# Ten units of seven half-size products a layer instead of nine in the feed-forward part of a two-layer decoder trunk in float32

## The chip, the cores and the metric

The kernel runs as one program on one core of a Trainium2 chip. The metric is the device time of one execution in microseconds (us); lower is better. Five engines run side by side, each working through its own list of instructions in order: TensorE (PE, with its weight loads shown as PEld), VectorE (DVE), ScalarE (ACT), GpSimd (POOL) and SyncE (SP). They meet only at semaphores. DMA queues move data between the chip's memory and the on-chip memory.

## The reference, cut to what matters

Each of two layers mixes (retention, spatial gating, dilated attention, an output product) and then runs a gated feed-forward block. The change touches the gate and up products of the last two lines:

```python
D_MODEL, SEQ, DEPTH, D_FF = 1024, 512, 2, 2816
for l in range(DEPTH):
    ...
    x = x + merged @ w_o[l]
    h = rms_norm(x, g_ffn[l])
    gate, up = jnp.split(h @ w_gate_up[l], 2, axis=-1)
    x = x + (jax.nn.silu(gate) * up) @ w_down[l]
```

Everything is float32, and h is 512 x 1024. Gate and up have 2816 columns each, that is 22 tiles of 128, which the kernel takes in 11 pairs of tiles.

## The kernel before, in words

**Float32 in parts.** Each operand of a product is stored as a high part (a copy in the type fp32r, which the matmuls read) and a low part (the rest). A product is three matmuls: high by high, high by low, low by high (L823, and L841 to L843). ACT makes the high part by a copy, DVE the low part by a subtraction. This holds for weights (`split_high` on ACT at L1011, `split_low` on DVE at L1215, per slab of 8 blocks of 128 x 128) and for activations.

**Tiles.** A layer is a list of tiles (`tiles_of_layer`), and tile i writes PSUM bank i modulo 2. So TensorE can't start tile i before tile i-2 has been read out of its bank (`wait_evacuated`). A plain gate or up tile (`fgate`, `fup`) is 8 blocks by 3 matmuls of 512 columns. For the first tile of the feed-forward block the normalization factor isn't ready, so plain tiles are computed from the gain-scaled x, and scaled afterwards by `norm_rstd` (L1322 for gate, L1355 and L1356 for up, where the second multiplies by the gate).

**Seven products.** A pair of gate tiles and a pair of up tiles together are a product of a 2 x 2 blocked input (halves of the tokens by halves of the 1024 inner columns) with a 2 x 2 blocked weight matrix. For a "quick" unit the kernel takes the seven products of Strassen's scheme (in Winograd's form) instead of eight. Each of the seven steps is one tile of 8 blocks by 3 matmuls of 256 columns:

```python
QUICK = (("a11", "b11"), ("s2", "t2"), ("a12", "b21"), ("s1", "t1"), ("s3", "t3"), ("s4", "b22"), ("a22", "t4"))
A11B11, S2T2, A12B21, S1T1, S3T3, S4B22, A22T4 = range(7)
ONTO = {A12B21: A11B11, S4B22: S1T1}
BY_SCALAR = (A11B11, A12B21, S1T1)
```

t1 to t4 are sums of weight blocks. POOL makes them ahead by adding DMAs in the chip's memory (L673, L675), eight DMAs a unit, one unit after the other, starting after the tile `rv 0` of the same layer. A11B11, A12B21 and S1T1 are read out by ACT (L1054 and L1064 are copies, L1060 is the silu), the other four by DVE (L1292 S2T2, L1295 and L1298 S3T3, L1301 and L1306 S4B22, L1308 A22T4). S2T2's read-out adds the copy of A11B11.

**Input of the units.** It is the same for all units of a layer, and made once, beside the plain tiles. DVE writes the normalized x (`normed`, 8 tiles, L1366), and the sums s1 to s4 of its quarters (`input_sum`, L1381; s2 from s1, and s4 from s2). ACT makes the high part of a11, a12, a22 and s1 to s4 (`part_high`, L1160), DVE the low part (`part_low`, L1386). In the first quick unit of a layer each of the seven tiles waits for the low part of its own input. The parts of a12 and a22 are stored over `h_high` and `h_low`, which plain tiles read, so their high parts wait for the last plain tile.

**Order.** `schedule` writes one list of steps by hand, and each engine takes its own instructions from it in that order. For tile i the list holds: the matmuls, `split_high` of the weights for the tile two further on, `pre[i]`, the read-out `evac`, `split_low`, and `post[i]`. The 4 gate and 4 up tiles of the 2 plain pairs come first (`PLAIN_PAIRS`), then units 2 to 5, then the down product over their 12 tiles, then units 6 to 10 and the second down product. SP loads slab s into one of 3 raw slots once slab s-3 has been split (L712); the slots of the split parts are 3 too.

Of the kernel before, what the change touches and what calls it, by code (L numbers as in the profile page):

```python
# [36 lines left out]
KT = D_MODEL // P  # L37
BLK = SEQ // P
FF_BLOCKS = (12, 10)
PLAIN_PAIRS = 2  # L40
PAIRS = D_FF // P // 2
QUICK_UNITS = range(PLAIN_PAIRS, PAIRS)
DILATIONS = ((128, 1), (512, 4), (2048, 16))
# [17 lines left out]
def tiles_of_layer():  # L61
# [18 lines left out]
    for half in range(2):  # L80
        if half == 0:
            for j in range(2 * PLAIN_PAIRS):
                t += [("fgate", 0, j), ("fup", 0, j)]
# [15 lines left out]
A11B11, S2T2, A12B21, S1T1, S3T3, S4B22, A22T4 = range(7)  # L99
# [4 lines left out]
AT = {t: i for i, t in enumerate(TILES)}  # L104
# [89 lines left out]
def schedule():  # L194
    pre = {i: [] for i in range(len(TILES))}
    post = {i: [] for i in range(len(TILES))}
# [43 lines left out]
    for n in range(KT):  # L240
        post[AT["proj", 1, n]] += [("high", "m", n), ("low", "m", n)]

        for tile, which in ((AT["wo", n], 1), (AT["down", 1, n], "next")):
# [3 lines left out]
            if n == KT - 1:  # L247
                pre[tile] += [("load_sqrt",)]
    for j in range(2 * PLAIN_PAIRS):
        post[AT["fup", 0, j]] += [("high", "f", 0, j), ("low", "f", 0, j)]  # L250
    for u in QUICK_UNITS:
        post[AT["quick", u, S4B22]] += [("high", "f1", u), ("low", "f1", u)]
        post[AT["quick", u, A22T4]] += [("second", u), ("high", "f2", u), ("low", "f2", u)]
    post[AT["fup", 0, 0]] += [("normed", n) for n in range(3)]
    post[AT["fgate", 0, 1]] += [("normed", n) for n in range(3, 7)]
    post[AT["fup", 0, 1]] += [("normed", 7), ("part_high", "a11"), ("part_low", "a11")]
    post[AT["fgate", 0, 2]] += [("input_sum", "s1"), ("input_sum", "s2"), ("part_high", "s2")]
    post[AT["fup", 0, 2]] += [("part_low", "s2"), ("part_high", "s1")]
    post[AT["fgate", 0, 3]] += [("part_low", "s1"), ("input_sum", "s3"), ("part_high", "s3")]
    post[AT["fup", 0, 3]] = [("part_high", "a12"), ("part_low", "s3")] + post[AT["fup", 0, 3]]  # L260
    post[AT["quick", PLAIN_PAIRS, A11B11]] += [("part_low", "a12")]
    post[AT["quick", PLAIN_PAIRS, S2T2]] += [("input_sum", "s4"), ("part_high", "s4"), ("part_low", "s4")]
    post[AT["quick", PLAIN_PAIRS, S1T1]] += [("part_high", "a22"), ("part_low", "a22")]

    post[AT["down", 1, KT - 2]] += [("fill_split",), ("split_high", "next", 0), ("split_low", "next", 0)]
    pre[AT["down", 1, KT - 1]] += [("split_high", "next", 1), ("split_low", "next", 1)]
# [32 lines left out]
STAT_AT, BCAST_AT = 3, 6  # L299
AFTER_NORM = (AT["k", 0, 0], AT["fgate", 0, 0])  # L300
STEPS = schedule()


# [1357 lines left out]
```

## Time and profile before

| | |
|---|---|
| median of 3 runs | 1927.08 us (1926.92 to 1927.63) |
| the profiled execution, its own time | 1928.07 us |
| its span in the profile | 1926.3 us |
| granted TensorE clock, mean | 0.999 of full speed |
| TensorE busy | 1902.9 us, 99% of the span |
| VectorE busy | 1236.6 us, 64% |
| ScalarE busy | 854.4 us, 44% |
| GpSimd busy | 97.0 us, 5% |

The profiled execution took 1.77 us more than its span, and lies 1.0 us over the median of the runs. Times of the trace count from the start of the span. Matmuls are pipelined and their ends are modelled in the rows, so the distance from one start to the next is what it takes of TensorE's time. In the same way the next instruction of DVE or ACT can start a little before the last has ended.

### The profile page before, as it was taken

How to read it: one execution, taken by the hardware profiler on the slowest of the kernel's cores; microseconds unless marked ns; L12 is line 12 of the kernel's file. 1: busy time of each engine (PE TensorE's matmuls, PEld its weight loads, DVE VectorE, ACT ScalarE, POOL GpSimd, SP SyncE). 2: the span in 40 equal slices, each digit the busy share in tenths (PEclk: the TensorE clock that was granted, in tenths of full speed). 3: DMA queues.
4: the chain of work that ended last, by engine and by line, in shares of the span. 5: the costliest groups of instructions: out<-in, count | busy, mean ns of one | idle time of the engine just before them, and what ended most of it. 6: DMA issues, size and time to landing. Idle time of an engine off the chain costs nothing. (4 is left out here: it accounts for less than half of the span.)

```text
span 1926.3 us, 26698 instructions
## 1 busy us (share of the span) xinstructions
PE 1902.9 (99%) x10664; PEld 1703.1 (88%) x10664; DVE 1236.6 (64%) x1633; ACT 854.4 (44%) x1194; POOL 97.0 (5%) x148
## 2 busy tenths in 40 slices
PE   7999999999999999999999999999999999999999
PEld 6888888888888899899888888888888888998998
DVE  6666756745666787267576666677366667863775
ACT  5444444434234455255445444344343344542554
POOL 0000001111111000000000000011111110000000
PEclk9999999999999999999999999999999999999999
DMA  5322247777777356356333222577777773553663
GB/s 190 83 81 84 78 121 197 192 207 202 214 206 198 99 158 182 102 183 198 122 108 87 74 78 79 138 198 188 216 193 199 200 206 106 176 157 109 204 204 126
DMA packets 85897, 295.68 MB, mean 153 GB/s; under 512 B 20368, under 2 KB 20624, under 8 KB 84624
## 3 DMA queue, kind: packets, MB, share of 16 engines
q1 hardware_dynamic: 73104, 218.49, 36.4%
q0 software_dynamic: 12672, 75.51, 17.3%
q8 instruction: 85, 1.39, 0.3%
q14 instruction: 36, 0.29, 0.1%
HBM read 291.79 MB, written 77.66 MB: 192 GB/s over the span
## 5 line engine op out<-in xcount | busy, mean ns | idle before, releaser
L1011 ACT ACTIVATE w_high<-raw 128x1024 fp32r<-128x1024 f32 x396 | 418.1, 1056 | 813.3 <-PE bank L823 685.7
L823 PE MATMUL bank<-h_high,w_high 128*128 128x512 f32 x1472 | 570.1, 387 | 12.8 <-DVE h_low L1220 11.3
L1215 DVE TENSOR_TENSOR w_low<-raw,w_high 128x1024 fp32r<-128x1024 f32 x396 | 482.8, 1221 | 123.3 <-ACT w_high L1011 117.5
L823 PE MATMUL bank<-h_low,w_high 128*128 128x512 f32 x1472 | 559.2, 380 | 0.0
L823 PE MATMUL bank<-h_high,w_low 128*128 128x512 f32 x1472 | 559.1, 380 | 0.0
L823 PEld LDWEIGHTS bank<-h_high,w_high 128*128 128x128 f32 x1472 | 279.2, 190 | 55.9 <-issue 9.4
L823 PEld LDWEIGHTS bank<-h_high,w_low 128*128 128x128 f32 x1472 | 279.0, 190 | 39.8
L823 PEld LDWEIGHTS bank<-h_low,w_high 128*128 128x128 f32 x1472 | 279.2, 190 | 38.3
L823 PE MATMUL bank<-in_high,w_high 128*128 128x512 f32 x672 | 255.0, 379 | 0.0
L823 PE MATMUL bank<-in_low,w_high 128*128 128x512 f32 x672 | 254.7, 379 | 0.0
L823 PE MATMUL bank<-in_high,w_low 128*128 128x512 f32 x672 | 254.7, 379 | 0.0
L1322 DVE TENSOR_TENSOR scaled<-bank,norm_rstd 128x512 f32<-128x512 f32 x128 | 93.7, 732 | 108.3 <-PE bank L823 107.8
L841 PE MATMUL bank<-s_high,w_high 128*128 128x256 f32 x576 | 158.4, 275 | 0.0
L842 PE MATMUL bank<-s_low,w_high 128*128 128x256 f32 x576 | 158.4, 275 | 0.0
L843 PE MATMUL bank<-s_high,w_low 128*128 128x256 f32 x576 | 158.4, 275 | 0.0
L823 PEld LDWEIGHTS bank<-in_high,w_high 128*128 128x128 f32 x672 | 127.0, 189 | 18.3 <-DVE in_low L1413 0.4
L823 PEld LDWEIGHTS bank<-in_high,w_low 128*128 128x128 f32 x672 | 127.0, 189 | 18.0
L823 PEld LDWEIGHTS bank<-in_low,w_high 128*128 128x128 f32 x672 | 127.0, 189 | 17.8
L843 PEld LDWEIGHTS bank<-s_high,w_low 128*128 128x128 f32 x576 | 110.6, 192 | 0.0
L842 PEld LDWEIGHTS bank<-s_low,w_high 128*128 128x128 f32 x576 | 110.6, 192 | 0.0
L841 PEld LDWEIGHTS bank<-s_high,w_high 128*128 128x128 f32 x576 | 110.6, 192 | 0.0
L1345 DVE TENSOR_TENSOR xT<-bank,xT 128x512 f32<-128x512 f32 x32 | 22.1, 691 | 125.3 <-PE bank L823 125.3
(156 smaller groups left out, 2253.1 us busy)
## 6 DMA issues: line engine op xcount, KB each, us to landing
raw<-weights SPq DMA_DIRECT2D x325, 512.0 KB, 4.0
weight_sums<-weights POOLq DMA_DIRECT2D x108, 512.0 KB, 6.1
raw<-weight_sums SPq DMA_DIRECT2D x72, 512.0 KB, 3.5
weight_sums<-weight_sums POOLq DMA_DIRECT2D x36, 512.0 KB, 4.0
turned<-rows SPq DMA_DIRECT2D x3, 768.0 KB, 7.0
xT<-x_t SPq DMA_DIRECT2D x8, 256.0 KB, 5.6
decay_sb<-decay SPq DMA_DIRECT2D x8, 256.0 KB, 4.5
out_t<-xT SPq DMA_DIRECT2D x8, 256.0 KB, 6.4
```

The source lines that it names most:

```text
L823: return pe.matmul(o, w, m, start=start, stop=stop)
L841: pe.matmul(part, wh, hi, start=k + c == 0 and not onto, stop=False, skip_group_check=onto)
L842: pe.matmul(part, wh, lo, start=False, stop=False, skip_group_check=onto)
L843: last = pe.matmul(part, wl, hi, start=False, stop=k == 3 and c == 1, skip_group_check=onto)
L1011: act.activation(w_high[:, PART_SLOT[s], :, :], raw[:, s % RAW_SLOTS, :, :], ACT.Copy).then_inc(part_high_w.sem, 1)
L1215: dve.tensor_tensor(w_low[:, PART_SLOT[s], :, :], raw[:, s % RAW_SLOTS, :, :], w_high[:, PART_SLOT[s], :, :], ALU.subtract).then_inc(part_ ...
L1322: dve.tensor_tensor(*operands, ALU.mult).then_inc(tile_stored.sem, 1)
L1345: dve.tensor_tensor(x, src.rearrange("p (t a i) -> p i a t", a=2, i=2), x, ALU.add).then_inc(tile_stored.sem, 1)
```

## The change

It sets `PLAIN_PAIRS` to 1. Gate and up tiles 2 and 3 of each layer are no longer plain tiles but a unit (unit 1) of seven products, first of ten. The down product reads the outputs of that unit in place of theirs. The host lays the weights out accordingly. The steps that make the units' input are spread over other tiles: before they stood behind six tiles of the plain eight, from `fup 0 0` to `fup 0 3`, and behind three of the first unit; now they stand behind three of four plain tiles and two of the first unit.

```diff
-PLAIN_PAIRS = 2
+PLAIN_PAIRS = 1
...
-    post[AT["fup", 0, 0]] += [("normed", n) for n in range(3)]
-    post[AT["fgate", 0, 1]] += [("normed", n) for n in range(3, 7)]
-    post[AT["fup", 0, 1]] += [("normed", 7), ("part_high", "a11"), ("part_low", "a11")]
-    post[AT["fgate", 0, 2]] += [("input_sum", "s1"), ("input_sum", "s2"), ("part_high", "s2")]
-    post[AT["fup", 0, 2]] += [("part_low", "s2"), ("part_high", "s1")]
-    post[AT["fgate", 0, 3]] += [("part_low", "s1"), ("input_sum", "s3"), ("part_high", "s3")]
-    post[AT["fup", 0, 3]] = [("part_high", "a12"), ("part_low", "s3")] + post[AT["fup", 0, 3]]
-    post[AT["quick", PLAIN_PAIRS, A11B11]] += [("part_low", "a12")]
-    post[AT["quick", PLAIN_PAIRS, S2T2]] += [("input_sum", "s4"), ("part_high", "s4"), ("part_low", "s4")]
-    post[AT["quick", PLAIN_PAIRS, S1T1]] += [("part_high", "a22"), ("part_low", "a22")]
+    post[AT["fup", 0, 0]] += [("normed", n) for n in range(5)]
+    post[AT["fgate", 0, 1]] += [("normed", n) for n in range(5, 8)]
+    post[AT["fgate", 0, 1]] += [("part_high", "a11"), ("part_low", "a11"), ("input_sum", "s1"), ("input_sum", "s2"),
+                                ("part_high", "s2")]
+    post[AT["fup", 0, 1]] = [("part_low", "s2"), ("part_high", "a12"), ("part_low", "a12")] + post[AT["fup", 0, 1]]
+    post[AT["fup", 0, 1]] += [("part_high", "s1"), ("part_low", "s1"), ("input_sum", "s3"), ("part_high", "s3")]
+    post[AT["quick", PLAIN_PAIRS, A11B11]] += [("part_low", "s3"), ("input_sum", "s4"), ("part_high", "s4")]
+    post[AT["quick", PLAIN_PAIRS, S2T2]] += [("part_low", "s4"), ("part_high", "a22"), ("part_low", "a22")]
```

## Rows read from the trace of the kernel before

**Rows 1.** The page: busy time, share of the span and instructions of each engine.

```profile
PE 1902.9 (99%) x10664; PEld 1703.1 (88%) x10664; DVE 1236.6 (64%) x1633; ACT 854.4 (44%) x1194; POOL 97.0 (5%) x148
```

**Rows 2.** Waits of PE, whole span: waiter, releaser, us in total, times, longest.

```profile
PE bank L823 <- DVE h_low L1220: 11.3, 5, 8.7
PE bank L841 <- issue: 3.5, 2, 1.7
...
PE bank L841 <- ACT sq L1054: 1.3, 2, 0.6
```

**Rows 3.** Timeline of PE, layer 0: start us, us, instruction, [idle before <-releaser].

```profile
661.73 0.38 PE L823 MATMUL bank<-h_high,w_high 128*128 128x512 f32 x1
...
682.45 0.27 PE L841 MATMUL bank<-a_high,w_high 128*128 128x256 f32 x1
...
687.70 0.28 PE L843 MATMUL bank<-s_high,w_low 128*128 128x256 f32 x1
689.71 0.35 PE L841 MATMUL bank<-h_high,w_high 128*128 128x256 f32 x1 [1.74 <-issue]
...
708.45 0.28 PE L843 MATMUL bank<-s_high,w_low 128*128 128x256 f32 x1
709.36 0.38 PE L841 MATMUL bank<-h_high,w_high 128*128 128x256 f32 x1 [0.64 <-ACT sq L1054]
```

**Rows 4.** Windows: us, busy of PE, PEld, DVE, ACT, POOL, clock, DMA share, GB/s.

```profile
661.70:682.40 20.70, 20.70 (x97) 18.12 (x97) 18.27 (x20) 9.98 (x12) 0.00 (x0) 1.00 0.34 109
682.40:703.20 20.80, 19.06 (x170) 18.88 (x169) 18.23 (x20) 12.98 (x16) 0.00 (x0) 1.00 0.47 134
722.80:741.60 18.80, 18.80 (x171) 18.80 (x170) 14.25 (x17) 10.66 (x13) 0.00 (x0) 1.00 0.65 199
```

**Rows 5.** Timeline of DVE beside the plain tiles of layer 0.

```profile
654.77 0.84 DVE L1410 TENSOR_TENSOR in_low<-prod,in_high 128x512 fp32r<-128x512 f32 x1
655.52 2.07 DVE L1366 SCALAR_TENSOR_TENSOR normed<-xT,vec,norm_rstd 128x512 f32<-128x512 f32 x3
657.51 0.68 DVE L1322 TENSOR_TENSOR scaled<-bank,norm_rstd 128x512 f32<-128x512 f32 x1
658.11 1.21 DVE L1215 TENSOR_TENSOR w_low<-raw,w_high 128x1024 fp32r<-128x1024 f32 x1
659.25 2.73 DVE L1366 SCALAR_TENSOR_TENSOR normed<-xT,vec,norm_rstd 128x512 f32<-128x512 f32 x4
661.93 0.69 DVE L1355 TENSOR_TENSOR tmp<-bank,norm_rstd 128x512 f32<-128x512 f32 x1
662.66 0.69 DVE L1356 TENSOR_TENSOR prod<-tmp,work 128x512 f32<-128x512 f32 x1
663.60 1.23 DVE L1215 TENSOR_TENSOR w_low<-raw,w_high 128x1024 fp32r<-128x1024 f32 x1 [0.24 <-DVE prod L1356]
...
666.16 1.21 DVE L1386 TENSOR_TENSOR a_low<-normed,a_high 128x1024 fp32r<-128x1024 f32 x1
...
669.41 1.22 DVE L1381 TENSOR_TENSOR input_sum<-normed 128x1024 f32<-128x1024 f32 x1
670.66 1.22 DVE L1381 TENSOR_TENSOR input_sum<-input_sum,normed 128x1024 f32<-128x1024 f32 x1
```

**Rows 6.** Timeline of ACT around the first unit of layer 0.

```profile
682.15 1.06 ACT L1160 ACTIVATE s_high<-normed 128x1024 fp32r<-128x1024 f32 x1 [3.04 <-DVE normed L1381]
683.12 1.05 ACT L1011 ACTIVATE w_high<-raw 128x1024 fp32r<-128x1024 f32 x1
...
686.59 0.58 ACT L1054 ACTIVATE sq<-bank 128x512 f32<-128x512 f32 x1
```

**Rows 7.** Timeline of POOL: the same issue in the last two rounds of layer 0.

```profile
577.07 0.81 POOL L673 DMA_DIRECT2D weight_sums<-weights  x1 [3.92 <-DMA weight_sums<-weight_sums]
...
614.51 0.81 POOL L673 DMA_DIRECT2D weight_sums<-weights  x1 [3.73 <-DMA weight_sums<-weight_sums]
```

**Rows 8.** Timeline of PE at the start of the kernel, behind its broken stretch.

```profile
18.76 0.61 PE L823 MATMUL bank<-h_low,w_high 128*128 128x512 f32 x1
...
22.15 0.40 PE L823 MATMUL bank<-h_high,w_high 128*128 128x512 f32 x1
```

## The prediction

> **What bounds the kernel now.** I read the busy shares first: TensorE is busy for 99% of the span, VectorE for 64%, ScalarE for 44% [rows 1]. So time comes off where TensorE has less to stream, and comes on wherever it has to wait. The list of its waits is the second view: 11.3 us at the start of the kernel, and then only a few, among them two of 1.7 us (3.5 in all) and two of 0.6 at the seven products [rows 2], one of each a layer. The timeline of TensorE says where these are [rows 3]. The plain tiles run without a break from 661.73 to 682.45. The first unit's A11B11 and S2T2 follow, then TensorE stands from 687.81 (687.70 plus one matmul of 0.11) to 689.71, 1.9 us, and its first pair is 0.1 slow: 2.0 in all. The second unit loses 0.8 at the same place (708.56 to 709.36). The windows [rows 4] show the other side: while the plain tiles 2 and 3 run, VectorE is busy for 18.27 us of 20.70, and in the first unit for 18.23 of 20.80, against 14.25 of 18.80 in a unit further on. It is there that the input of the units is made. VectorE, hardly noticed on the page, is nearly full in just the stretch from which the change takes tiles.
>
> **Less streaming.** A plain pair is 4 tiles x 24 matmuls = 96. From 661.73 to 682.45 there are 96, so 0.2158 us each and 20.72 a pair [rows 3]. A unit is 7 x 24 = 168 matmuls of 256 columns. The first 48 go from 682.45 to 687.81, 0.1117 each [rows 3]; a unit is 18.76, which the undisturbed window confirms (171 starts in 18.80) [rows 4]. The difference is 1.96 us a layer, 3.9 for both. The Trainium skill ("TensorE: Matmul & The Clock Gate", Back-to-back issue gap) gives columns by 2.4 GHz plus 2.5 ns, 109.2 ns for 256 columns; the trace disagrees with 111.7. By the page a unit would be 18.3 us and the gain 4.7 instead of 3.9. I take the rows.
>
> **Other work of the extra unit.** A unit has 14.25 us of VectorE and 10.66 of ScalarE under 18.80 of TensorE [rows 4], and each is free for the rest, so it costs nothing in the steady stretch. The three more slabs a layer bring three more loads by SP, one per tile of 2.7 us, into slots that wait for VectorE's split, so they are early where VectorE is late. POOL makes a tenth round of sums: 37.4 us [rows 7]. Its rounds now end some 6 us behind 614.51, then at about 658, and the tenth unit's weights are wanted after more than 100 us of further tiles, so this is hidden; the new first unit's sums are made first of all. If that cover were gone the cost would be the 37 us, but nothing points to it. I take 0 for all of this.
>
> **The moved preparation.** This is the main term. Before, the parts for A11B11 had until 682.45. Now TensorE has finished `fup 0 1` at 661.73 and wants them there, 20.7 us sooner. Nothing of VectorE's preparation is dropped. I therefore walk the new list from the point where both agree, 655.5 [rows 5]. The pitches, start to start, are from rows 5: 0.66 a `normed` (four in 2.68), 0.6 a read-out of a gate tile, 1.14 a weight split or a low part, 1.2 a sum, 1.66 the two instructions of an up tile until the next can start (661.93 to 663.60), 0.75 a plain tile's low part. On ScalarE a high part or weight split has a pitch of 0.97 and a duration of 1.06, a copy out of a bank takes 0.58 [rows 6].
>
> 1. VectorE: five `normed` to 658.8, gate read-out to 659.4, weight split to 660.6, three `normed` to 662.6, low part of a11, done at 663.8. ScalarE has the high part long before. **A11B11 starts at 663.9 instead of 661.7: 2.1 us of wait.** It ends at 666.6.
> 2. VectorE: s1 at 663.7, s2 at 664.9, which ends at 666.1. Only then comes the read-out of `fup 0 1` (ready since 661.9) to 667.7. ScalarE, which is held by s2, makes its high part from 666.2 and the weight split from 667.1 to 668.2. VectorE: weight split at 668.2, low part of s2 at 669.3, done at 670.6. **S2T2 starts at 670.7, having been possible at 666.6: 4.0.** It ends at 673.4.
> 3. VectorE: low part of a12 at 670.5, of the plain product at 671.6, of s1 at 672.4, sum s3 from 673.5 to 674.7. On ScalarE the high part of s3 stands behind that sum, and behind it, in order, are the weight split and the copy of A11B11 out of its bank, which A12B21 needs: 674.8, 675.7, and the copy from 676.7 to 677.3. **A12B21 starts at 677.4: 4.0.** It ends at 680.1. The added wait is thus one of ScalarE for VectorE's sum, with TensorE queued behind the copy.
> 4. VectorE: weight split at 676.8 (held by ScalarE), low part of s3 at 677.9, sum s4 at 679.1, and only then the read-out of S2T2, from 680.3 to 681.0, though ready since 673.5. **S1T1, which writes the same bank, starts at 681.1: 1.0.** It ends at 683.8.
> 5. ScalarE: high part of s4 at 680.4, then two weight splits and the high part of a22, and the silu of A12B21 from 684.2 to 684.8. **S3T3 starts at 684.9: 1.1.** The rest of the unit has what it wants and ends at 693.0.
>
> The waits sum to 12.2 in the first unit. In the second the wait for the copy stays; I take 0.3, from 0 and the 0.8 of before. That is 12.5 against 2.8 before, 9.7 more a layer, of which the streaming gives back 2.0. A layer grows by 7.8, and since both layers have the same rows, the kernel by 15.6. TensorE has nothing left beside these stretches that could take the delay in. 1928.07 + 15.6 = 1943.7 for the execution that was profiled. The median of the runs is 1.0 lower, so I forecast **1942.7 us**.
>
> **A bound from both sides.** Of the trace, nothing shows how ScalarE and VectorE interleave in the new order. Where ScalarE held up nobody, VectorE's own list would still set S1T1's start: less 0.5 at its split at 668.2 and 2.1 at the one at 676.8. S1T1 would start at 678.5, and S3T3 at most 1.1 sooner still, so 3.7 less a layer: +4.1, or +8 for both. From above: each of the dozen hand-overs of the walk may take 0.1 more, 1.2 a layer.
>
> **Rivals.** *The clock falls.* At the start TensorE had waits of 0.3 to 1.5 us between 13 and 18.5, then the matmuls from 18.76 to 22.15 ran at 0.43 us each, 8 of them, in which 15.7 would have run at 0.216 [rows 8]: 1.7 us lost, at the lower of the two levels, 1.2 instead of 2.4 GHz. Waits of 4.0 us are longer. But of the five tiles of the walk the first four are followed by a wait: S2T2, slowed by 1.7, ends at 675.1, before 677.4, and A12B21 ends at 681.8, 0.7 behind S1T1's start, which the wait of 1.1 behind S1T1 takes back. So in the likeliest case it costs nothing. If a low stretch falls on S3T3 and what follows, 1.7 a layer come on top: 1946.1. The Trainium skill (same page, Why this matters for your kernels) warns that idle gaps between bursts bring the clock back to half; no row of the middle of this kernel shows it, since the wait of 1.9 us left the granted clock at 1.00 [rows 4].
>
> *VectorE's list alone counts*, ScalarE is in time: the bound above, 1927.1 + 8 = 1935 at the extreme, about 1939 if half of it holds.
>
> *The preparation is hidden, and the kernel is faster.* The place is A11B11 to A12B21: their parts would have to be there at 661.7, 664.4 and 667.1. Then the waits of the first unit stay as before and 3.9 come off: 1923.2. It needs VectorE to be done with s2's low part 6.2 us sooner than the walk says. Against it: VectorE has hardly a gap in the walk to 674, and 18.27 of 20.70 were busy with this before [rows 4].
>
> *It doesn't do what it says*: the constant is used wherever tiles, sources and units are listed, so this has no share.
>
> **How the numbers follow.** Forecast 0.76; clock 0.12; VectorE alone 0.09; hidden 0.03. The forecast's own spread is the hand-overs, -1.5 to +2.4. The range goes from 1938, by the bound without ScalarE's part, to 1947, by the clock. A difference under 0.2% (3.9 us) is about what a measurement of this kernel can't tell from none. The hidden case lies at that edge, so it gives 0.02 to faster and 0.01 to the same; the other three are all slower, 0.97.
>
> **What would show it.** In the profile after: TensorE's list of waits gets about 20 us longer, at the seven products alone; per layer waits of about 2, 4, 4, 1 and 1 us before the first five tiles of unit 1, for VectorE's low parts (L1386) and ScalarE's copy (L1054); VectorE without a break from 655 to 674; units from the third on 18.8 us apart; 96 fewer matmuls of 512 columns at L823 and 56 more at each of L841 to L843 in a layer. It is wrong if A11B11 follows `fup 0 1` at once, if the wait before A12B21 is short, or if waits show at later units.

## The result, and the profile after

The changed kernel takes 1943.06 us, median of 4 runs (1942.69 to 1945.36), against 1927.31 us before (4 runs, the three of the table above and one more): a ratio of 1.0085, 95% interval 1.007 to 1.01. It is 15.8 us slower. 1942.7 us was forecast.

The first lines of the page of the changed kernel (busy time, share, instructions; against [rows 1]):

```profile
span 1940.9 us, 27042 instructions
...
PE 1907.2 (98%) x10808; PEld 1712.1 (88%) x10808; DVE 1244.3 (64%) x1641; ACT 861.4 (44%) x1204; POOL 108.2 (6%) x164
```

144 more matmuls: 112 more on each of the three lines of the seven products (336), less 192 of 512 columns. VectorE's and ScalarE's totals hardly move. These totals don't say why the kernel is slower; the waits do.

Waits of TensorE in the changed kernel, whole span (waiter, releaser, us in total, times, longest; against [rows 2]; its line numbers are 2 lower from L258 on):

```profile
PE bank L839 <- issue: 10.2, 4, 3.9
PE bank L821 <- DVE h_low L1218: 10.1, 3, 8.2
PE bank L839 <- ACT sq L1052: 4.9, 3, 2.2
...
PE bank L839 <- ACT work L1058: 0.5, 2, 0.3
```

At the seven products the list grew from 4.8 to 15.6 us. Where they are, and which tile they delay, the timeline of TensorE in the changed kernel shows, layer 0 (start, us, instruction, idle before; against [rows 3]):

```profile
660.30 0.38 PE L821 MATMUL bank<-h_high,w_low 128*128 128x512 f32 x1
662.66 0.35 PE L839 MATMUL bank<-a_high,w_high 128*128 128x256 f32 x1 [1.98 <-issue]
...
665.30 0.28 PE L841 MATMUL bank<-a_high,w_low 128*128 128x256 f32 x1
669.49 0.55 PE L839 MATMUL bank<-s_high,w_high 128*128 128x256 f32 x1 [3.91 <-issue]
...
673.53 0.28 PE L841 MATMUL bank<-s_high,w_low 128*128 128x256 f32 x1
675.97 0.58 PE L839 MATMUL bank<-h_high,w_high 128*128 128x256 f32 x1 [2.16 <-ACT sq L1052]
...
680.30 0.28 PE L839 MATMUL bank<-s_high,w_high 128*128 128x256 f32 x1
...
682.87 0.28 PE L841 MATMUL bank<-s_high,w_low 128*128 128x256 f32 x1
683.43 0.38 PE L839 MATMUL bank<-s_high,w_high 128*128 128x256 f32 x1 [0.28 <-ACT work L1058]
...
697.92 0.38 PE L839 MATMUL bank<-h_high,w_high 128*128 128x256 f32 x1 [0.83 <-ACT sq L1052]
...
730.26 0.28 PE L839 MATMUL bank<-a_high,w_high 128*128 128x256 f32 x1
```

Here `fup 0 1` ends at 660.52. In the kernel before it ended at 661.73; the 1.2 us come from the start of the kernel: one and the same wait ends at 27.97 in the kernel before and at 26.75 here, since the first wait is 0.5 shorter (8.2 against 8.7) and the clock stayed at 1.00 where it was at 0.66 before (window 18 to 23). The walk of the prediction, less 1.2, stands beside the rows:

| tile of the first unit | walk less 1.2 | start measured | us that TensorE lost before it |
|---|---|---|---|
| A11B11 | 662.7 | 662.66 | 2.1 |
| S2T2 | 669.5 | 669.49 | 4.1 |
| A12B21 | 676.2 | 675.97 | 2.3, and 1.5 in S2T2 by the clock |
| S1T1 | 679.9 | 680.30 | none, but 1.7 in A12B21 by the clock |
| S3T3 | 683.7 | 683.43 | 0.5 |

The losses sum to 12.2 us, as in the walk. In layer 1 the first unit lost as much: from the end of `fup 0 1` to the start of S4B22 are 25.68 us there and 25.69 in layer 0.

The last row printed starts the fourth unit (730.26). From the end of `fup 0 1` to it are 69.74 us, over three units. The same tiles of the kernel before, one plain pair and two units, ran from 661.73 to the start of its third unit at 722.87: 61.14 us. The layer grew by 8.6. In layer 1 the same stretch grew by 7.7 (1622.56 to 1691.38 against 1615.20 to 1676.33). 16.3 less the 1.2 at the start, and 0.5 less behind the last of these points, is the 14.6 by which the span grew.

VectorE in the changed kernel, beside the last plain tiles and the first unit (timeline; against [rows 5]), has one gap between 652.5 and 673.3:

```profile
654.31 3.40 DVE L1364 SCALAR_TENSOR_TENSOR normed<-xT,vec,norm_rstd 128x512 f32<-128x512 f32 x5
...
661.34 1.22 DVE L1384 TENSOR_TENSOR a_low<-normed,a_high 128x1024 fp32r<-128x1024 f32 x1
662.48 1.22 DVE L1379 TENSOR_TENSOR input_sum<-normed 128x1024 f32<-128x1024 f32 x1
663.73 1.23 DVE L1379 TENSOR_TENSOR input_sum<-input_sum,normed 128x1024 f32<-128x1024 f32 x1
664.87 0.68 DVE L1353 TENSOR_TENSOR tmp<-bank,norm_rstd 128x512 f32<-128x512 f32 x1
665.59 0.69 DVE L1354 TENSOR_TENSOR prod<-tmp,work 128x512 f32<-128x512 f32 x1
667.02 1.23 DVE L1213 TENSOR_TENSOR w_low<-raw,w_high 128x1024 fp32r<-128x1024 f32 x1 [0.74 <-ACT w_high L1009]
668.17 1.22 DVE L1384 TENSOR_TENSOR s_low<-input_sum,s_high 128x1024 fp32r<-128x1024 f32 x1
```

The low part of a11 ends at 662.56 and A11B11 starts at 662.66; the low part of s2 ends at 669.39 and S2T2 starts at 669.49. The rows of TensorE put both waits down to "issue", which means that the profile shows no releaser; these times show it. ScalarE's timeline shows the step that holds A12B21 (against [rows 6], where the same high part cost nothing):

```profile
673.43 1.06 ACT L1158 ACTIVATE s_high<-normed 128x1024 fp32r<-128x1024 f32 x1 [4.00 <-DVE normed L1379]
674.39 1.04 ACT L1009 ACTIVATE w_high<-raw 128x1024 fp32r<-128x1024 f32 x1
675.34 0.58 ACT L1052 ACTIVATE sq<-bank 128x512 f32<-128x512 f32 x1
```

It waits 4.0 us for VectorE's sum s3, with the weight split and the copy of A11B11 behind it in its list. The copy of A11B11 (L1052) ends at 675.92, A12B21 starts at 675.97.

### The profile page after: what moved, and what is told of

Read it like the earlier page. It is cut to its first block and busy times, and to the rows that moved or that the text cites. A ratio compares the mean times of both kernels' runs of the same rounds, so it can differ in the third digit from the quotient of the medians.

```text
span 1940.9 us, 27042 instructions
## 1 busy us (share of the span) xinstructions
PE 1907.2 (98%) x10808; PEld 1712.1 (88%) x10808; DVE 1244.3 (64%) x1641; ACT 861.4 (44%) x1204; POOL 108.2 (6%) x164
## 5 line engine op out<-in xcount | busy, mean ns | idle before, releaser
L821 PE MATMUL bank<-h_high,w_high 128*128 128x512 f32 x1408 | 545.5, 387 | 11.6 <-DVE h_low L1218 10.1
L821 PE MATMUL bank<-h_high,w_low 128*128 128x512 f32 x1408 | 534.6, 380 | 0.0
L821 PE MATMUL bank<-h_low,w_high 128*128 128x512 f32 x1408 | 534.6, 380 | 0.0
L821 PEld LDWEIGHTS bank<-h_high,w_high 128*128 128x128 f32 x1408 | 266.9, 190 | 52.3 <-issue 8.8
L839 PE MATMUL bank<-s_high,w_high 128*128 128x256 f32 x640 | 178.0, 278 | 6.7 <-issue 6.2
L840 PE MATMUL bank<-s_low,w_high 128*128 128x256 f32 x640 | 177.3, 277 | 0.0
L841 PE MATMUL bank<-s_high,w_low 128*128 128x256 f32 x640 | 177.3, 277 | 0.0
L839 PEld LDWEIGHTS bank<-s_high,w_high 128*128 128x128 f32 x640 | 124.3, 194 | 7.4 <-issue 6.5
L840 PEld LDWEIGHTS bank<-s_low,w_high 128*128 128x128 f32 x640 | 124.4, 194 | 0.0
L841 PEld LDWEIGHTS bank<-s_high,w_low 128*128 128x128 f32 x640 | 124.2, 194 | 0.0
```

Of the source, the lines that this page charges most:

```text
L821: return pe.matmul(o, w, m, start=start, stop=stop)
L839: pe.matmul(part, wh, hi, start=k + c == 0 and not onto, stop=False, skip_group_check=onto)
L840: pe.matmul(part, wh, lo, start=False, stop=False, skip_group_check=onto)
L841: last = pe.matmul(part, wl, hi, start=False, stop=k == 3 and c == 1, skip_group_check=onto)
```

## The experiments

**Is the preparation what is late?** e1 takes most of it out of the changed kernel, e2 out of the kernel before. Their output leaves out three quarters of the units' input.

```diff
-dve.tensor_tensor(input_source(name), a, b, op).then_inc(input_summed.sem, 1)
+dve.tensor_tensor(input_source(name)[:, 0:1, :], a[:, 0:1, :], b[:, 0:1, :], op).then_inc(input_summed.sem, 1)
...
-hi, lo = in_turn(high[:, k, :]), in_turn(low[:, k, :])
+hi, lo = in_turn(high[:, 0, :]), in_turn(low[:, 0, :])
```

(part_high and part_low likewise; six of eight `normed` for 16 columns.) In e1 two steps also stand elsewhere in the list, the low part of s2 and the high part of s3, as the expectation says.

e1, expected: 

> The changed kernel with the preparation of the units' input nearly taken out: sums, high parts and low parts are made for a quarter of the columns only, six of the eight normalized tiles for 16 columns each, and the seven products read that quarter four times (so streaming, weight splits and read-outs stay whole). Part_low of s2 stands ahead of the read-out of fup 0 1 and part_high of s3 behind the copy of A11B11. Theory (the preparation is what is late): no wait is left at the first two units, 12.8 us a layer less than the changed kernel, so about 1917.5 us, and 9.8 us less than the kernel before. Rival (a unit more costs by itself, by its loads, sums or read-outs): waits stay at later units or at A11B11, and the time stays over 1925 us.

Measured: 1920.60 us, but 8 runs from 1917.73 to 1924.39; ratio to the kernel before 0.9967 (0.9956 to 0.9977).

e2, expected: 

> The kernel before with the same preparation taken out in the same way, its order unchanged. Theory: the wait of 2.0 us before A12B21 falls to about 0.3 us and that in the second unit shrinks to some tenths, so about 1922 us. Against e1 it lacks the shorter streaming of the extra unit: e1 is lower by 3.9 us plus what is left of these waits (0.4 a layer), 4 to 5 us. Rival (the streaming gain isn't real): e1 and e2 within 1 us.

Measured: 1922.32 us, 9 runs within 0.8 us; 0.9976 (0.9965 to 0.9986), as expected. So without its preparation, and with these two steps moved, the changed kernel is 22.5 us faster: its 15.8 us are gone, and more. But e1 was 3 us over the forecast with an odd spread, and its profile has a wait in layer 1 alone. ScalarE's timeline of e1 says for what:

```profile
1622.93 1.06 ACT L1009 ACTIVATE w_high<-raw 128x1024 fp32r<-128x1024 f32 x1 [3.12 <-DMA raw<-weight_sums]
```

a slab that landed late. GpSimd's tenth round of sums had run into the first unit, which starts at 1609.96 in layer 1; its last issues in e1 (timeline of POOL):

```profile
1609.76 0.52 POOL L673 DMA_DIRECT2D weight_sums<-weight_sums  x1 [6.34 <-DMA weight_sums<-weights]
1614.57 0.81 POOL L671 DMA_DIRECT2D weight_sums<-weights  x1 [4.30 <-DMA weight_sums<-weight_sums]
```

In layer 0 of e1 the last issue was at 656.74, the first unit started at 661.16, and nothing waited.

**Is it the tenth round?** e5 and e9 are e1 with that round put elsewhere, by one wait on GpSimd:

```diff
                     t1, t2, t3, t4 = (sums_dram[layer, n, w] for w in range(4))
+                    if n == len(QUICK_UNITS) - 1:
+                        pool.wait_ge(tile_done.sem, tile_done.at(layer * STRIDE, AT["quick", PLAIN_PAIRS, A22T4]))
```

e5, expected: 

> e1 with one wait added on GpSimd: the tenth round of weight sums of a layer starts only once the first unit is done. In e1 that round ran into the first unit, loads of weight sums landed in 4.5 us instead of 3.4, and the runs spread over 6.7 us. Theory (the spread and the excess over 1917.5 are this round's traffic on the DMA engines): median 1917.5 us within 1 us, spread under 1.5 us. Rival (the spread has another source, such as the extra unit itself): it stays at some 1920 us with a spread of several us.

Measured: 1931.16 us (1929.37 to 1933.71): 11 us worse than e1. Both the theory and the rival of the expectation missed: my place for the round was the wrong one. It ran from 680.17 to beyond 718.29, beside the second and third unit; the same stretch of e5, and of e9 below (windows as in [rows 4]):

```profile
680.00:723.00 43.00, 38.65 (x337) 37.85 (x336) 28.25 (x33) 20.77 (x27) 5.37 (x8) 1.00 0.86 255
```

```profile
680.00:723.00 43.00, 43.00 (x386) 43.00 (x385) 32.89 (x38) 25.06 (x32) 0.00 (x0) 1.00 0.63 197
```

The loads of that stretch, in e5 first and then in e9 (DMA issues: count, KB each, median us from issue to landing):

```profile
raw<-weight_sums SPq DMA_DIRECT2D x8, 512.0 KB, 6.2
...
raw<-weights SPq DMA_DIRECT2D x6, 512.0 KB, 6.2
```

```profile
raw<-weight_sums SPq DMA_DIRECT2D x8, 512.0 KB, 4.0
raw<-weights SPq DMA_DIRECT2D x7, 512.0 KB, 4.3
```

An estimate from these rows: a slab's round through one of three slots is its landing, 1.06 us of high part and 1.22 of low part. With 4.0 to 4.3 that is some 6.5 us, inside the 8.0 of three tiles of 2.68; with 6.2 it is 8.5, more than TensorE leaves, and in e5 TensorE waits.

e9, expected: 

> e1 with the tenth round of weight sums moved to the first down product of the layer, where the loads of weights are far apart, instead of the plain tiles and the first unit (e1) or the second unit (e5, 1931 us). Theory (a unit's loads, one per 2.7 us into three slots, bear no other traffic on the DMA engines): no wait at any unit, median 1917.5 us within 1 us, spread under 1.5 us, 5 us less than e2. Rival (the tenth unit costs a few us wherever its sums are made): 1920 us or more.

```diff
-tile_done.at(layer * STRIDE, AT["quick", PLAIN_PAIRS, A22T4])
+tile_done.at(layer * STRIDE, AT["down", 0, 0])
```

Measured: 1917.67 us (1916.82 to 1917.89), ratio 0.9951 (0.9937 to 0.9966), without a wait at any unit. It lies 4.65 us below e2, of the 4 to 5 expected: the extra unit's shorter streaming is real. It also lies 2.9 us below e1, and its runs spread over 1.1 us instead of 6.7: e1's excess and spread were this round.

**Does the round cost the changed kernel anything?** e6 is the changed kernel with the wait of e5, e10 with that of e9.

e6, expected: 

> The changed kernel itself with the tenth round of sums started behind the first unit. Theory: VectorE and ScalarE are later than the loads in the first unit, so the tenth round's traffic is hidden there: 1943 us within 0.7 us, and at most the single high run of the changed kernel (1945.4 us) is explained by it. Rival (the late loads are part of the loss): 1 to 4 us less.

Measured: 1957.53 us (1956.32 to 1958.92), 14.5 more than the changed kernel, where neither the theory (no change) nor the rival (less) had a rise: again the second unit is the wrong place.

e10, expected: 

> The changed kernel with the tenth round in the first down product. Theory: in the changed kernel this round is hidden by the plain tiles and by the long waits of the first unit, so 1943 us within 1 us, against 1957.5 us with the round in the second unit (e6). Rival (the round costs the changed kernel some us where it lies): 1939 to 1941 us.

Measured: 1944.11 us (1942.69 to 1945.00), within the runs of the changed kernel: nothing gained. Where the change leaves the round, beside the plain tiles and the waiting first unit, it costs the changed kernel nothing.

**Which part has ScalarE's order?** e3 moves one step of the changed kernel:

```diff
-    post[AT["fup", 0, 1]] += [("part_high", "s1"), ("part_low", "s1"), ("input_sum", "s3"), ("part_high", "s3")]
-    post[AT["quick", PLAIN_PAIRS, A11B11]] += [("part_low", "s3"), ("input_sum", "s4"), ("part_high", "s4")]
+    post[AT["fup", 0, 1]] += [("part_high", "s1"), ("part_low", "s1"), ("input_sum", "s3")]
+    post[AT["quick", PLAIN_PAIRS, A11B11]] += [("part_high", "s3"), ("part_low", "s3"), ("input_sum", "s4"), ("part_high", "s4")]
```

Expected: 

> The changed kernel with one step moved: part_high of s3 behind the copy of A11B11 on ScalarE. Theory (both VectorE's list and ScalarE's order): A12B21 starts with no wait, but S1T1 then waits for VectorE's read-out of S2T2, which comes 2.1 us sooner and no more, so 2.1 us a layer less, about 1938.9 us. Rival (VectorE's list alone sets the end): no change, 1943 us. Rival (the wait before A12B21 costs its full length): 4 us a layer less, 1935 us.

Measured: 1939.97 us (1939.74 to 1940.21), 3.1 less than the changed kernel. The timeline of TensorE in e3, the first unit's last three waits:

```profile
669.75 0.35 PE L839 MATMUL bank<-s_high,w_high 128*128 128x256 f32 x1 [2.29 <-issue]
...
677.79 0.38 PE L839 MATMUL bank<-s_high,w_high 128*128 128x256 f32 x1 [0.82 <-DVE scaled L1290]
681.61 0.38 PE L839 MATMUL bank<-s_high,w_high 128*128 128x256 f32 x1 [0.87 <-DVE s_low L1384]
```

The wait before A12B21 is gone, and S1T1 waits instead for VectorE's read-out of S2T2 (L1290). The first row shows only 2.29 because A11B11 ran at the lower clock in this execution and ended at 667.29; S2T2 starts as late behind `fup 0 1` as before. The last row names the low part of s4, which S3T3 doesn't read; ScalarE's silu of A12B21, which frees its bank, ended at the same time (681.56).

Neither rival holds: not all 4 us a layer came back, and not none. The total is 1.1 us short of the forecast, the first unit is not: from the end of `fup 0 1` to the start of S4B22 e3 takes 23.64 us in both layers, 2.05 less than the changed kernel, where 2.1 was expected. In the profiled execution 0.3 was lost again in the second unit of layer 0, and 0.9 behind the last matmul (its start to the end of the span is 4.9 us in e3, 4.0 in the changed kernel).

**The clock.** e4 fills the two long waits with matmuls nobody reads:

```diff
                 last.then_inc(tile_done.sem, 1)
+                if u == PLAIN_PAIRS and step in (A11B11, S2T2):
+                    for _ in range(32):
+                        pe.matmul(score_bank[0][:, 0:2 * P], ones_r[:, :], in_turn(a11_high[:, 0, :]), start=True, stop=True)
```

Expected: 

> The changed kernel with 32 further matmuls of 256 columns (3.6 us at the upper clock) into an unused bank behind A11B11 and behind S2T2 of the first unit, so that TensorE's two long waits are filled and its granted clock stays at 1.00 there. Theory (the low clock is hidden by the waits behind it): the time stays at 1943 us within 1 us. Rival (the fall of the clock costs): up to 1.7 us a layer for each low stretch that isn't hidden, 1936 to 1940 us.

Windows of the changed kernel, then of e4 (the number behind the five engines is the granted clock):

```profile
668.00:671.00 3.00, 1.51 (x7) 1.55 (x8) 3.00 (x4) 1.43 (x2) 0.00 (x0) 0.67 0.98 239
671.00:675.00 4.00, 2.81 (x19) 2.62 (x18) 2.40 (x3) 1.57 (x2) 0.00 (x0) 0.82 0.11 43
675.00:678.00 3.00, 2.03 (x9) 2.04 (x10) 2.54 (x3) 0.91 (x2) 0.00 (x0) 0.64 0.16 23
```

```profile
668.00:671.00 3.00, 2.67 (x24) 2.50 (x23) 3.00 (x4) 1.55 (x2) 0.00 (x0) 1.00 0.53 150
671.00:675.00 4.00, 4.00 (x38) 4.00 (x38) 2.48 (x3) 1.49 (x2) 0.00 (x0) 1.00 0.06 23
675.00:678.00 3.00, 2.94 (x26) 2.75 (x26) 2.45 (x3) 1.00 (x2) 0.00 (x0) 1.00 0.15 18
...
1625.00:1628.00 3.00, 3.00 (x17) 3.00 (x16) 2.49 (x3) 1.76 (x2) 0.52 (x1) 0.51 0.29 57
```

Measured: 1943.01 us (1942.08 to 1943.27) against 1943.06. In layer 0 of the changed kernel the clock fell to the lower level, 1.2 GHz, behind both long waits, as the Trainium skill warns ("TensorE: Matmul & The Clock Gate", Why this matters for your kernels); in layer 1 it fell behind the first wait too (0.50 from 1625 to 1628). That wait is 2.1 us in both layers, and in layer 0 no fall followed it, so the wait of 1.9 us that the prediction took for harmless says little. The filler kept it at 2.4 GHz in layer 0 only; in layer 1 A11B11 still ran at the lower level, as the last row shows, and the filler behind it put S2T2 off by 1.1 us. So layer 0 is the test, and there the first unit is no faster at 2.4 GHz: 25.75 us from the end of `fup 0 1` to the start of S4B22, against 25.69. In e4 the wait before S1T1 stands in the timeline again, 0.70 us for VectorE's read-out, and S3T3's is 0.87 instead of 0.28. What TensorE lost by its clock it would have waited.

**Is it the order, or VectorE's load?** e7 and e11 have one plain pair, with the steps in the order that the walk found best (below, but for the eight `normed`, which come as early as they can); e7 has the wait of e5 and e11 that of e9 on GpSimd. e8 has two plain pairs, so treated too.

```diff
...
+    post[AT["fgate", 0, 1]] = [("normed", 5), ("normed", 6), ("normed", 7), ("input_sum", "s1"), ("part_high", "a11")] + post[AT["fgate", 0, 1]]
+    pre[AT["fup", 0, 1]] = [("input_sum", "s2"), ("part_low", "a11"), ("part_high", "a12"), ("part_high", "s2"), ("part_high", "a22")] + pre[AT["fup", 0, 1]]
+    post[AT["fup", 0, 1]] += [("part_high", "s1"), ("part_low", "s2"), ("part_low", "s1"), ("input_sum", "s3")]
+    post[AT["quick", PLAIN_PAIRS, 0]] = [("part_high", "s3")] + post[AT["quick", PLAIN_PAIRS, 0]]
+    pre[AT["quick", PLAIN_PAIRS, 1]] = [("part_low", "a12")] + pre[AT["quick", PLAIN_PAIRS, 1]]
+    post[AT["quick", PLAIN_PAIRS, 1]] = [("input_sum", "s4"), ("part_low", "s3"), ("part_high", "s4"), ("part_low", "a22")] + post[AT["quick", PLAIN_PAIRS, 1]]
+    post[AT["quick", PLAIN_PAIRS, 2]] = [("part_low", "s4")] + post[AT["quick", PLAIN_PAIRS, 2]]
```

e7, expected: 

> One plain pair, with the preparation steps in another order, found by walking VectorE's and ScalarE's lists with the durations of the trace: part_high and part_low of a11 behind all eight normalized tiles and s1, part_low of a12 and s3 and all of s4 later, the read-out of fup 0 1 behind s2 and a11; tenth round of sums late, as in e6. Theory (waits come from the order and from VectorE's load together): waits of about 3.7, 1.9 and 1.8 us before A11B11, S2T2 and A12B21 and none behind, 7.4 us a layer instead of 12.5, 10 us less in all: about 1933 us, still above the kernel before. Rival (only the order was at fault): at or below 1925 us.

Measured: 1949.30 us (1947.11 to 1951.60), 16 over the forecast. It had the tenth round in the second unit, which cost 14.5 us in e6, and so tells nothing of the order.

e11, expected: 

> e7 with the tenth round in the first down product, so that the order of the preparation is seen by itself. Theory (VectorE's load and its order together): waits of about 3.7, 1.9 and 1.8 us in the first unit and none behind, about 1933 us, 10 us less than the changed kernel and still above the kernel before. Rival (only the order was at fault): at or below 1925 us.

Measured: 1932.64 us (1932.31 to 1933.54), ratio to the kernel before 1.0031 (1.0019 to 1.0042). Its waits in layer 0, from the timeline of TensorE:

```profile
664.39 0.35 PE L843 MATMUL bank<-a_high,w_high 128*128 128x256 f32 x1 [3.66 <-issue]
668.92 0.49 PE L843 MATMUL bank<-s_high,w_high 128*128 128x256 f32 x1 [0.35 <-issue]
673.47 0.35 PE L843 MATMUL bank<-h_high,w_high 128*128 128x256 f32 x1 [1.49 <-issue]
```

A11B11 ran at the lower clock here (0.66 from 664.3 to 669), so the wait before S2T2 shows as 0.35; by the starts TensorE lost 3.8, 1.85 and 1.87 us, as expected. That is 7.5 a layer against 2.8 before, and with the shorter streaming 5.7 us more than the kernel before. Two thirds of the loss was the order; the rest stays in the best order that I found.

e12 exchanges two low parts in the kernel before:

```diff
-    post[AT["fup", 0, 3]] = [("part_high", "a12"), ("part_low", "s3")] + post[AT["fup", 0, 3]]
-    post[AT["quick", PLAIN_PAIRS, A11B11]] += [("part_low", "a12")]
+    post[AT["fup", 0, 3]] = [("part_high", "a12"), ("part_low", "a12")] + post[AT["fup", 0, 3]]
+    post[AT["quick", PLAIN_PAIRS, A11B11]] += [("part_low", "s3")]
```

Expected: 

> The kernel before with two steps exchanged: the low part of a12 ahead of the low part of s3, which goes behind A11B11. Theory (VectorE's list is full, a wait only moves): A12B21 no longer waits, but S3T3 waits 2.0 us behind ScalarE's and VectorE's later steps, and only the wait in the second unit shrinks: 0.4 us a layer less, about 1926.3 us. Rival (the one late low part was the whole loss): 4 us less, 1923 us.

Measured: 1926.36 us (1925.81 to 1927.08), ratio 0.9997 (0.9988 to 1.0006). TensorE in e12, layer 0, has no wait before A12B21 any more, and this one before S3T3:

```profile
694.54 0.38 PE L841 MATMUL bank<-s_high,w_high 128*128 128x256 f32 x1 [1.72 <-ACT work L1060]
```

The wait only moved, since ScalarE's read-out of A12B21 stands behind its high part of s4, and that behind VectorE's sum.

e8 goes after all of them: the parts of a12 first, the sums s3 and s4 earlier, and no copy of ScalarE behind a step that waits for a sum. Ahead of `fup 0 1` two of seven `normed` are gone to later tiles and the high part of a11 stands sooner; from there on the list reads:

```diff
...
+    post[AT["fup", 0, 1]] += [("part_low", "a11"), ("normed", 5), ("normed", 6)]
+    post[AT["fgate", 0, 2]] += [("normed", 7), ("input_sum", "s1"), ("part_high", "s1"), ("input_sum", "s2"), ("part_high", "s2"), ("input_sum", "s3"), ("part_low", "s2")]
+    post[AT["fgate", 0, 3]] += [("part_high", "s3"), ("part_low", "s1")]
+    pre[AT["fup", 0, 3]] = [("input_sum", "s4")] + pre[AT["fup", 0, 3]]
+    post[AT["fup", 0, 3]] = [("part_high", "a12"), ("part_low", "a12")] + post[AT["fup", 0, 3]]
+    pre[AT["quick", PLAIN_PAIRS, 1]] = [("part_high", "a22"), ("part_low", "s3")] + pre[AT["quick", PLAIN_PAIRS, 1]]
+    post[AT["quick", PLAIN_PAIRS, 1]] = [("part_high", "s4"), ("part_low", "s4")] + post[AT["quick", PLAIN_PAIRS, 1]]
+    pre[AT["quick", PLAIN_PAIRS, 3]] = [("part_low", "a22")] + pre[AT["quick", PLAIN_PAIRS, 3]]
```

Expected: 

> The kernel before (two plain pairs) with its preparation steps in another order: the parts of a12 ahead of the low part of s3, the sums s3 and s4 some tiles sooner, and the copies on ScalarE not held by them. Theory: both waits (2.0 and 0.8 us a layer) go, TensorE runs through: 1927.1 less 5.6 to 5.9, about 1921.3 us. Rival (the waits are at the loads or the banks): 1925 to 1927 us.

Measured: 1921.49 us, 6 runs from 1920.83 to 1921.77, ratio 0.9971 (0.9959 to 0.9982): 5.4 us faster than the kernel before and 21.6 faster than the changed one. Behind the wait at the start of the kernel, the longest waits of TensorE in e8 are these:

```profile
PE bank L933 <- ACT work L1192: 1.6, 2, 0.8
PE bank L825 <- DVE work L1327: 0.8, 2, 0.4
PE bank L825 <- DVE scaled L1324: 0.4, 2, 0.2
```

There is none at the seven products.

## Why the prediction was right, point by point

**Less streaming, -3.9.** Right. e9 against e2 gives 4.65, where 3.9 and up to 0.8 of small waits were expected. The starts account for it: for the same output tiles e2 takes 58.74 us, with a plain pair and two units (661.20 to 719.94, and as long in layer 1), and e9 56.42, with three units (660.53 to 716.95, 56.43 in layer 1), which is 2.3 less a layer. Of that, 0.4 is what e2 loses at its first A12B21, of which its list of waits shows 0.2. The rest, 1.9 a layer or 3.8 in all, is the streaming. The 4.7 that the prediction worked out from the Trainium skill ("TensorE: Matmul & The Clock Gate", Back-to-back issue gap) is an estimate for the streaming alone (4.8 without its rounding), and too high: the three units of e9 take 18.81 us each, so its matmuls of 256 columns start 0.112 us apart, not 0.109. The prediction took the 171 of [rows 4] for starts in 18.80 us; the number counts also the matmuls that began before the window, and 168 of them take that time.

**The moved preparation, +19.4 for both layers.** Right in kind and size. The five starts of the first unit came within 0.4 us of the walk. Taking the preparation out, with two steps and the tenth round moved (e9), brings the changed kernel from 1943.06 to 1917.67 us; the round's place alone gains nothing (e10).

**ScalarE queued behind VectorE's sum.** Right, shown by e3: moving it removed that wait, and as the walk had it, VectorE's own list then held S1T1. The gain was 3.1 us rather than 4.2, though 2.05 a layer in the first unit itself, as expected.

**The waits one by one.** Some were wrong in form. I had 4.0 before A12B21, 1.0 before S1T1 and 1.1 before S3T3, and measured 2.3, none and 0.5; the rest had become slow matmuls. The list of waits therefore grew by 10.8 us and not by about 20. The time was the same, because each tile's start was set by VectorE or ScalarE. The clock's rival was right that the clock falls and wrong on the price. e4 shows the price to be nil in layer 0, where the bound was 1.7 a layer; in layer 1 it could not test it, but the first unit took the same 25.68 us there.

**The second unit, 0.3.** In layer 0 it measured 1.0, where ScalarE had waited 3 us for a slab; in layer 1 nothing. That is why the layers grew by 8.6 and 7.7 around the 7.8 of the walk.

**The rest of the extra unit, 0.** The result holds, the reason was too broad. I had the tenth round end at 658 and called it hidden. Its last issue was at 665.30, at the end of the first unit's A11B11, and in layer 1 at 1616.13, just ahead of `fup 0 1` (timeline of GpSimd):

```profile
665.30 0.81 POOL L671 DMA_DIRECT2D weight_sums<-weights  x1 [4.67 <-DMA weight_sums<-weight_sums]
```

e10 shows that it costs nothing there. But e5 and e6 show that it costs 13.5 and 14.5 us once it falls on a unit in full stream, and e1 that it costs 3 us in its present place as soon as the preparation is not the later of the two. "Cover" for a transfer is not only the time until its data is wanted; it is also what shares the DMA engines with it.

**The hidden case, for which 0.03 was set**, did not come. e11 says what it lacked: the best order that I found still leaves 5.7 us more than the kernel before. The order came from a walk of the lists, and nothing shows that no better one exists.

**The number itself.** 0.4 us off is closer than the working deserves. The sum has a slip of 0.1 a layer (9.7 less 2.0 is 7.7, not 7.8). The second unit cost 0.7 more than assumed in layer 0 and 0.3 less in layer 1. The spans of the two profiled executions differ by 14.6, of which -1.2 is the start of the kernel, where the two programs are the same. And the 1.0 from the profiled execution to the median was carried over from the kernel before; the changed kernel's profiled execution lies 0.4 below its median. What holds beyond luck are the first unit's 12.2 us, in both layers.

What stays open: whether e3's longer stretch behind the last matmul belongs to the kernel or to the one execution, and whether moving some sums to GpSimd would let one plain pair win. Neither was tried.

## What to carry to other kernels

Work that hides another engine's preparation has a price when it is cut: before replacing slow tiles by fast ones, write out the list of the engine that prepares beside them, with the pitches of the trace, and see when each input is ready. An engine at 64% over the whole span can be full in the one stretch that counts. Then look at the order of that list before giving up tiles. Here the gain of 5.4 us lay in the order, with the number of tiles left as it was.

## What the runs showed of the hardware that I had not expected

Adding DMAs in the chip's memory beside a stream of weight loads cost more here than their bytes suggest. One round of eight (512 KB each) over some 43 us brought the DMA share from 0.63 to 0.86 only, yet the loads' landing rose from 4.0 and 4.3 to 6.2 us, and the kernel lost 13.5 us over the two rounds (e5 against e9). What the loads wait for there, the DMA engines or the memory, no run shows.

TensorE at the lower clock hid inside waits: in layer 0 the granted clock was 0.64 to 0.82 from 668 to 678, and with 1.00 there (e4) the first unit took the same time to 0.1 us.
